# A hybrid decoder step on one Trainium2 core: the attention layer's samples on four column groups, its value projection in three rounded passes, units begun inside it

## What is computed

```python
def qkv_heads(h, pos, w_qkv, q_gain, k_gain):
    qkv = (h @ w_qkv).reshape(Bt, S, N_GROUPS, 3, N_HEADS, HEAD_DIM)   # 3 groups, 8 heads of 64
    q = rope_partial(rms_norm(qkv[:, :, :, 0], q_gain), pos)
    k = rope_partial(rms_norm(qkv[:, :, :, 1], k_gain), pos)
    return q, k, qkv[:, :, :, 2]
...
# prompt: banded causal attention per group (window, dilation) = (128,1), (512,4), (2048,16)
# sample: each of 8 sequences attends to its cached keys (128, 128 and 64 reachable per query) and 4 new ones
# both: softmax over the three groups' scores joined by their denominators, then @ w_o
```

## Time and profile before

| | us |
|---|---|
| median of 3 runs | 2732.45 (2731.07 to 2735.79) |
| the profiled execution's own time | 2726.56 |
| its span, first to last instruction | 2724.7 |
| PE busy in the span | 2538.6 (93%) |
| DVE, ACT, POOL busy | 1612.4, 947.1, 783.1 |
| mean granted TensorE clock | 0.958 of full speed |
| 680 stream tiles, 512 KB each, from issue to landing | 3.3 |
| a cached key or value tile, 1792 KB | 7.9 or 7.4 |

### The profile page before, as it was taken

How to read it: one execution, slowest core, us unless ns; L and a number is a source line. 1 busy time by engine, 2 the same in 40 slices (tenths; PEclk the granted TensorE clock), 3 DMA queues, 4 the chain that set the end, 5 groups by cost and what they waited for, 6 DMA issues and landing times.

```text
span 2724.7 us, 47969 instructions
## 1 busy us (share of the span) xinstructions
PE 2538.6 (93%) x17164; PEld 2233.2 (82%) x17164; DVE 1612.4 (59%) x3417; ACT 947.1 (35%) x1627; POOL 783.1 (29%) x586
## 2 busy tenths in 40 slices
PE   5698889999999999999699898899999999999998
PEld 2244779999999999999684334579999999999998
DVE  7999537978898433333441112247968898333333
ACT  1122334344444444444220101034344443444443
POOL 0388726840000222222440000037830000222222
PEclk7699999999999999999799897899999999999999
DMA  8463334443333544444433442034443334444444
GB/s 306 175 217 138 121 126 151 153 137 131 124 131 134 169 166 165 164 167 163 176 109 116 178 161 82 31 134 155 145 141 127 127 128 144 165 166 163 168 162 141
DMA packets 104968, 405.74 MB, mean 149 GB/s; under 512 B 12560, under 2 KB 12816, under 8 KB 101680
## 3 DMA queue, kind: packets, MB, share of 16 engines
q1 hardware_dynamic: 98064, 357.74, 38.3%
q10 hardware_dynamic: 6816, 46.91, 4.6%
HBM read 395.46 MB, written 9.14 MB: 148 GB/s over the span
## 4 chain that ended last, share of the span: by engine, by line
PE 59%; issue 22%; POOL 9%; DVE 8%; ACT 1%; DMA 0%; ACTq 0%; POOLq 0%; DVEq 0%
PE ps L1099 10%; PE ps L1091 10%; PE ps L1095 10%; POOL ring_lo L1685 7%; PE ps L1071 6%; PE ps L1070 6%; PE ps L1074 6%; PE ps L1058 5%; DVE big L1406 2%; POOL ring_lo L1692 1%; PE ps L629 1%; PE ps L969 1%; PE ps L633 1%; PE ps L636 1%; PE ps L965 1%
## 5 line engine op out<-in xcount | busy, mean ns | idle before, releaser
L298 ACT ACTIVATE wt_hi<-ring 128x1024 fp32r<-128x1024 f32 x552 | 581.0, 1053 | 318.2 <-PE ps L969 209.2
L1606 DVE TENSOR_TENSOR ring_lo<-ring,wt_hi 128x1024 fp32r<-128x1024 f32 x256 | 314.7, 1230 | 492.1 <-ACT wt_hi L298 492.1
L1703 POOL TENSOR_TENSOR split<-big,w_hi 128x288 fp32r<-128x288 f32 x256 | 208.1, 813 | 1201.7 <-PE ps L1074 603.3
L1685 POOL TENSOR_TENSOR ring_lo<-ring,wt_hi 128x1024 fp32r<-128x1024 f32 x112 | 307.9, 2756 | 127.5 <-ACT wt_hi L298 127.5
L1070 PE MATMUL ps<-split,wt_hi 128*128 128x288 f32 x1152 | 328.5, 307 | 0.0
L1071 PE MATMUL ps<-split,wt_hi 128*128 128x288 f32 x1152 | 316.1, 298 | 0.0
L1099 PE MATMUL ps<-w_hi,ring_lo 128*128 128x288 f32 x2048 | 313.1, 295 | 1.4 <-DVE ring_lo L1606 1.4
L1095 PE MATMUL ps<-split,wt_hi 128*128 128x288 f32 x2048 | 313.1, 295 | 0.3
L1091 PE MATMUL ps<-w_hi,wt_hi 128*128 128x288 f32 x2048 | 312.9, 295 | 0.0
L1099 PEld LDWEIGHTS ps<-w_hi,ring_lo 128*128 128x128 f32 x2048 | 285.4, 188 | 1.9 <-DVE ring_lo L1606 1.9
L1095 PEld LDWEIGHTS ps<-split,wt_hi 128*128 128x128 f32 x2048 | 285.4, 188 | 0.8 <-POOL split L1703 0.8
(11 more groups left out here) (276 smaller groups left out, 3724.3 us busy)
## 6 DMA issues: line engine op xcount, KB each, us to landing
ring<-in_stream SPq DMA_DIRECT2D x680, 512.0 KB, 3.3
big<-in_kc ACTq DMA_DIRECT2D x8, 1792.0 KB, 7.9
big<-in_vc ACTq DMA_DIRECT2D x8, 1792.0 KB, 7.4
out_qk<-big ACTq DMA_DIRECT2D x1, 3456.0 KB, 10.3
x_keep<-xT ACTq DMA_DIRECT2D x2, 1152.0 KB, 5.5
xT<-x_keep ACTq DMA_DIRECT2D x2, 1152.0 KB, 5.8
out_v<-big ACTq DMA_DIRECT2D x1, 1536.0 KB, 13.9
xT<-in_xT ACTq DMA_DIRECT2D x1, 1152.0 KB, 9.2
```

What stands on the lines that cost most here:

```text
L298: nc.scalar.activation(wt_hi[:, n % 2], ring[:, n % RING], ACT.Copy).then_inc(S["hi_ready"], 1)
L1606: TT(ring_lo[:, s], ring[:, s], wt_hi[:, s % 2].bitcast(F32), ALU.subtract)\
L1685: TT(ring_lo[:, s], ring[:, s], wt_hi[:, s % 2].bitcast(F32), ALU.subtract)\
L1703: TT(w_lo[:, s % 2], W[:, bass.ds(4 * i + s, 1), :].rearrange("p a t -> p (a t)"), w_hi[:, s % 2].bitcast(F32), ALU.subtract).then_inc(S[" ...
```

## The change

All in the attention layer; the reference's mathematics stays the same.

- **Start.** ACT rounds the first two weight tiles, issues 22 loads of constants (the last part of the sample mask in 16 pieces) and four key loads, and only then calls `root_mean(2)`.
- **Queries and keys.** ACT copies each bank by itself behind its tile (24 copies instead of 6), and PE waits for the one bank that it writes next. DVE still squares four banks at once.
- **Values.** The prompt's products are made in three rounded passes (`v_tile`); the low part of even tiles comes from DVE (`low_v`), of odd ones from POOL (`low_odd`). The 32 sample tokens' products stay plain and go, four at a time, to four groups of 32 columns (`v_samples`), whose four partial sums are added by one product with a constant (`v_sum`) that also puts the group's rows in place.
- **Samples.** The 128 PSUM partitions now stand for head pairs, not for sequences: the four head pairs of a batch go to four column groups (`sample_keys`, `sample_values`), the sequences lie beside each other. The values of a batch are 28 calls of 128 columns instead of 7 of 512. The new keys and values are taken once for each half; `qz` is laid out anew (`spread_q`), the result copied by ACT (`sample_out`) instead of DVE.
- **Order.** The first half's softmax, its turn, units 0 and 1 and the scores of units 2 and 3 stand inside the value tiles. The 16 units run on without a break between the halves, and the samples' batches are spread behind units 2 to 15 (`SAMPLE_AT`). PSUM banks are dealt out anew so that units, samples and values don't share any, and a fourth buffer takes the fourth key load.

```diff
-LOV = (0, GROUPS + 128)
+LOV = (0, 6 + GROUPS + 128)
+IN_ATT = 16 * 22
+SAMPLE_AT = {2: 6, 4: 7, 8: 8, 9: 9, 10: 10, 12: 11, 14: 12, 15: 13}
+VBANK = ((0, 2), (3, 5), (0, 2))
...
-        def attention_act(act, own):
+        def attention_act(act, root_mean):
             act.wait_ge(S["tile_done"], VT[0] + 128)
+            high(act, QK)
+            high(act, QK + 1)
...
+            for q in range(HP):
+                for b in range(4):
+                    act.dma_start(smaskv[32 * q + 8 * b:32 * q + 8 * b + 8, CK:SW + 96],
+                                  I["smaskv"][32 * b:32 * b + 8, CK:SW + 96]).then_inc(S["in_att"], 16)
...
-            for n in range(3):
+            for n in range(4):
                 load_kv(n)
+            root_mean(2)
...
-                nc.scalar.activation(qk[:, 4 * gs:4 * gs + 4, :], ps[:, 0:4, 0:T], ACT.Copy)\
-                   .then_inc(S["aq_copied"], 1)
...
+            for n in range(24):
+                act.wait_ge(S["tile_done"], QK + n + 1)
+                high(act, QK + n + 2)
+                nc.scalar.activation(qk[:, n, :], ps[:, n % 4, 0:T], ACT.Copy).then_inc(S["aq_copied"], 1)
+                if n >= 4 and n % 4 == 0:
+                    qk_root(n // 4 - 1)
...
             for gs in range(6):
-                if gs:
-                    pe.wait_ge(S["aq_copied"], gs)
                 for m in range(4):
+                    if gs:
+                        pe.wait_ge(S["aq_copied"], 4 * gs + m - 3)
                     qk_tile(4 * gs + m, ps[:, m, 0:T])
...
+            def v_samples(g, pr):
+                n0 = VP + 4 * g + 2 * pr
+                for n in (n0, n0 + 1):
+                    tile_wait(pe, n)
+                for j in range(4):
+                    n, z = n0 + j // 2, j % 2
+                    ins = mm(ps[32 * j:32 * j + 32, VBANK[g][1], :], modsq[:, 4 * pr + j, 256:T],
+                             ring[:, n % RING, 512 * z:512 * z + 512], start=(pr == 0), stop=(pr == 1))
+                ins.then_inc(S["v_small"], 1)
+            def v_tile(g, s):
+                n, b = VP + 4 * g + s, VBANK[g][0]
+                pe.wait_ge(S["hi_ready"], HI[0] + 280 + 4 * g + s + 1)
+                for z in range(2):
+                    w = wt_hi[:, n % 2, 512 * z:512 * z + 512]
+                    for x in (h_hi, h_lo):
+                        for a in range(2):
+                            mm(ps[:, b + a, :], x[:, 2 * s + z, 128 * a:128 * a + 128], w,
+                               start=(s == 0 and z == 0 and x is h_hi), stop=False)
...
+            def sample_keys(n):
+                hf, b = n // 8, n % 4
+                kb = kv(n).rearrange("p (q k) -> p q k", q=HP)
+                for g in range(NG):
+                    bank, c0 = (6, 0) if g == 1 else (7, KOFF[g] - 512)
+                    for q in range(HP):
+                        ins = mm(ps[32 * q:32 * q + 32, bank, c0:c0 + NK[g]], qz[:, g, hf, q, 32 * b:32 * b + 32],
+                                 kb[:, q, KOFF[g]:KOFF[g] + NK[g]], start=(b == 0 and g < 2),
+                                 stop=(b == 3 and g == 1), skip_group_check=True)
...
+            def sample_values(n):
...
+                for k in range(7):
+                    for q in range(HP):
+                        ins = mm(ps[32 * q:32 * q + 32, 6, 128 * b:128 * b + 128], pts[:, k, 32 * q:32 * q + 32],
+                                 vb[:, k, 128 * q:128 * q + 128], start=(b == 0 and k == 0), stop=False,
+                                 skip_group_check=True)
...
+            for j in range(12):
+                g, s = j // 4, j % 4
+                if j == 4:
+                    pe.wait_ge(S["aq_done"], 6)
+                    pe.wait_ge(S["qz_ready"], NG)
+                    for n in range(4):
+                        sample_keys(n)
+                    sample_new_keys(0)
+                    v_sum(0)
...
+                if s % 2 == 0:
+                    v_samples(g, s // 2)
+                v_tile(g, s)
+                if j == 0:
+                    norm(5)
+                if j == 1:
+                    spread_out(5)
+                if j == 2:
+                    rotate(5)
+                if j == 6:
+                    sample_turn(0)
+                if j == 8:
+                    v_sum(1)
+                    unit_scores(0)
+                    unit_scores(1)
+                if j == 9:
+                    sample_values(4)
+                if j == 10:
+                    unit_turn(0)
+                    unit_scores(2)
+            unit_turn(1)
+            unit_scores(3)
+            sample_values(5)
+            v_sum(2)
+            unit_pv(0)
+            for u in range(2, 16):
+                unit_turn(u)
+                if u + 2 < 16:
+                    unit_scores(u + 2)
+                unit_pv(u - 1)
+                if u in SAMPLE_AT:
+                    n = SAMPLE_AT[u]
...
+                    (sample_values if n % 8 >= 4 else sample_keys)(n)
...
+                if u == 12:
+                    sample_new_keys(1)
+                if u == 13:
+                    sample_turn(1)
+            unit_pv(15)
+            sample_values(14)
+            sample_values(15)
+            sample_new_values(1)
+            sample_fold(1)
...
+            low_v(0)
             scale_qk(5)
+            low_v(1)
             finish(5)
...
+            low_v(2)
+            sample_max(0)
+            sample_norm(0)
+            low_v(3)
+            low_v(4)
+            unit_max(0)
+            unit_max(1)
+            low_v(5)
+            for u in range(16):
+                unit_den(u)
+                if u + 2 < 16:
+                    unit_max(u + 2)
+                if u:
+                    unit_out(u - 1)
+                if u == 12:
+                    sample_max(1)
+                if u == 13:
+                    sample_norm(1)
```

More of the change, by code:

```diff
@@ L504, in unit_t @@
                     act.wait_ge(S["us_pv"], u - 1)
[L505 to L520 removed]
+                nc.scalar.activation(pt_sb[u % 2][:, 0:w], unit_turned(u)[:, 0:w], ACT.Copy)\
+                    .then_inc(S["us_cpa"], 1)
@@ new lines, in v_tile @@
+            def v_tile(g, s):
[7 more added lines that the diff above has]
+                               start=(s == 0 and z == 0 and x is h_hi), stop=False)
+                if s % 2:
+                    pe.wait_ge(S["lo_u"], LOU[0] + PRE + 24 + 2 * g + s // 2 + 1)
+                else:
+                    pe.wait_ge(S["lo_v"], LOV[0] + GROUPS + 128 + 2 * g + s // 2 + 1)
+                for z in range(2):
+                    for a in range(2):
+                        ins = mm(ps[:, b + a, :], h_hi[:, 2 * s + z, 128 * a:128 * a + 128],
+                                 ring_lo[:, n % RING, 512 * z:512 * z + 512], start=False, stop=(s == 3 and z == 1))
+                ins.then_inc(S["tile_done"], 1)
@@ new lines, in sample_new_keys @@
+            def sample_new_keys(hf):
+                for g in range(NG):
+                    c0 = NEWC - 512 + 32 * g
+                    for b in range(4):
+                        for q in range(HP):
+                            ins = mm(ps[32 * q:32 * q + 32, 7, c0:c0 + 32], qz[:, g, hf, q, 32 * b:32 * b + 32],
+                                     qk[:, 8 * g + 4 + q, 256:T], start=False, stop=(b == 3 and g == NG - 1),
+                                     skip_group_check=True)
+                ins.then_inc(S["ss_mm"], 1)
@@ L748, in sample_pv, with sample_new_values @@
-                if bb == 3:
-                    ins.then_inc(S["ss_pv"], 1)
+            def sample_new_values(hf):
+                pe.wait_ge(S["vn_copied"], NG)
+                for b in range(4):
+                    for q in range(HP):
+                        ins = mm(ps[32 * q:32 * q + 32, 6, 128 * b:128 * b + 128], pts[0:96, 7, 32 * q:32 * q + 32],
+                                 v_new[0:96, 128 * q:128 * q + 128], start=False, stop=(b == 3), skip_group_check=True)
+                ins.then_inc(S["ss_pv"], 1)
@@ L1118, in attention_dve, with low_v @@
                                nc.vector.tensor_copy)
-            v.wait_ge(S["in_att"], 80)
+            v.wait_ge(S["in_att"], IN_ATT)
+            def low_v(s):
+                n = VP + 2 * s
+                v.wait_ge(S["hi_ready"], HI[0] + 280 + 2 * s + 1)
+                v.wait_ge(S["v_small"], s + 1)
+                TT(ring_lo[:, n % 4], ring[:, n % 4], wt_hi[:, n % 2].bitcast(F32), ALU.subtract)\
+                    .then_inc(S["lo_v"], 1)
             def finish(gs):
```

376 lines of the change are left out of this document (185 added, 191 removed).

## The result

| | before | after |
|---|---|---|
| median, us | 2733.15 (4 runs) | 2582.86 (4 runs, 2582.37 to 2583.46) |
| the profiled execution's own time, us | 2726.56 | 2582.37 |
| its span, us | 2724.7 | 2580.6 |
| mean granted clock | 0.958 | 0.962 |

A forecast was written before the change was run, and what follows sets the result against it. PE's own instructions bound the value stage; sample work and a PE-DVE-ACT chain the units. Value stage and units 306 to 86 + 104 = 190, -116, +1.9: -114 us; 2726.56 - 114 = 2612.6, against the median 2618, range 2590 to 2660.

The forecast's parts named there:

- rival (e): Second PEER stage: its granted clock falls behind the denser attention layer, making the kernel slower, 2776 us; chance 0.03.
- rival (d): Units begun early in the value stage gain nothing, 15 us comes back: 2633 us; chance 0.07.
- rival (c): Value batches: 128-column products do not overlap on the groups, a batch stays at 6.2 us, 39 less saved: 2657; chance 0.06.
- The wait at the norm: Query and key tiles: PE reaches the norm before DVE's square is done, a new 1.5 us wait per group.
- the third POOL subtract: Layer start: POOL runs a third subtract right behind the second, so one more DVE modulate step waits: +2.0 us.
- The clock allowances: Low-clock time added: 7 us in the value stage (79 to 86), and units 2 to 15 taken at 104, not 90.
- the list at high clock: Units 2 to 15 priced one by one at PE's high clock: 90 us, of it units 2 to 7 28.
- rival (a): Value stage and units all at high clock, 79 + 90 us, a saving of 135: 2597 us; chance 0.15.
- The four-group calls: Value stage sample work on four column groups: key batch 1.9 us, value batch 1.9, new keys left at 3.4.
- The start: Layer start: issues ahead of ACT's root cost +4.4 us, a DVE step waiting for POOL +2.0; taken 6.4.
- The query and key tiles: Bank waits and slow tiles go, new norm waits come, two slow tiles stay: -4.5 us, between -9 and +2.
- rival (b): Units at low clock throughout, 90 + 147 us for both stages, a saving of 67: 2665 us; chance 0.12.

The follow-up runs named there:

- e4: Kernel after, with units 0 to 2 and sample 4's value batch moved behind the last value tile instead of between the tiles: 2589.5 us.
- e8: Kernel after, with all sample work from unit 2 on moved into one block behind unit 15; one execution: 2625.0 us.
- e12: Second value batch and new values moved from behind unit 4 to behind unit 6, on a kernel with plain value products, later POOL start and later norm (2575.4): 2577.8 us.
- e11: Kernel after, with the first half's second value batch and new values moved from behind unit 4 to behind unit 6: 2579.6 us.
- e1: Kernel after, with the four head pairs of the sample batches one behind the other, so successive calls write the same column group: 2609.6 us.
- e2: Kernel after, with the prompt's value tiles as plain f32 products, without their rounded copies and low-part subtracts: 2581.2 us.

## Why the prediction was wrong in size

**What held.** PE's work was the bound, and the column groups took it away; the second PEER stage did not slow (rival (e): 1.00 from 2060 to 2580 us); the units did begin inside the value tiles (rival (d), priced at 15 us; 6.7 in e4); and value products of 128 columns do overlap (rival (c)): a batch takes 1.74 us on four groups and 5.08 one group behind the other. The wait at the norm (1.5, measured 1.63), the third POOL subtract (+2.0, measured +2.0) and the rounded tile (2.84, measured 2.90 to 2.99) were sized well.

**What failed, of the 30 us that the sum missed.**

1. *The clock allowances, 7 us in the value stage and 14 in the units*, the step that failed. In the value stage the low clock cost 1.7 us in one stretch. In the units the largest part was units 2 to 7: they were taken as low mostly, 35 us where the list at high clock has 28, and took 27.7, with a granted clock of 1.00 from 1508 to 1528. The reading behind it, 0.59 where units ran without samples, did not hold everywhere: short units without samples ran low in e8 and e12 and at 1.00 in e11. So why they stayed high in the kernel after is open; that units 2 and 4 have a value batch behind them is not shown to be the reason. The list at high clock, 90 us, came within 1.3 of the measured 91.3, but by luck. The measured time holds two low stretches that the list does not. They are worth 5 to 6 us, an estimate: unit 8 took 7.81 where unit 9, with more products, took 5.50; units 13 and 14 took 15.4 together and 13.1 in e4, where the clock rose earlier; and e11's units took 84.9 in all. The list itself was too long by nearly as much: unit 12 stood at 13, with new keys at 3.4, and took 9.9. For the same reason rival (a), all high clock, came nearest (169 us for the two stages; 166.2 measured; chance 0.15) although 27 us of the units ran low.
2. *The four-group calls, 4 to 5 us in the value stage.* New keys were left at the price of one group, 3.4, and took 0.88: 96 instructions on four groups go at 9 ns each, a quarter of the old 0.035 us. Key batches were priced from a quad of 512 columns at 1.9 and took 1.5.
3. *The start, 3.5 us.* A full issue (0.485) was taken for a small mask piece and 0.68 for a key load; 0.367 and 0.51 were measured (2.4 us in all), and the issues began 1.1 us earlier against the PEER stage's end.
4. *The query and key tiles, 3.4 us.* Two slow tiles were left in (2.8); behind the norms there was none. Of the three slow tiles of before only two started at 2.29 for eight products; the third fell later in the tile, and its cost was much the same (4.9 us instead of 3.4).

Against these stand waits that the prediction's clock of the value stage had shorter: tile 2 ended 20.2 us behind the last key tile, not 17.5. The 2 us of waits that it put among tiles 4 to 7 were not there. Two of its figures don't follow from its terms, though little hangs on them: 36, 13.3 and 2 give 51.3 without the turn's 1.6, not 51.5, and the 90 us of the value stage in rival (b) have no working.

The forecast also lost 5 us by its basis: the profiled execution of before lay 6 below the median, and the prediction added these 6 to its sum, while the profiled execution after lies at its median.

The range ended at 2590, below the rival without any low clock (2597); but that rival kept the terms of points 2 to 4, which all erred to the same side.

## What to carry to other kernels

Small products that use 32 of PE's columns are worth spreading over the four column groups with neighbouring instructions on different groups, and here narrow ones gained too: a batch cost a third to a quarter of its price on one group (1.74 against 5.08 us, 1.72 against 6.22). Work for which PE has room in the waits of a chain belongs there: the samples cost under 1 us inside the units against 42 behind them. And a forecast that lists its terms at the high clock should carry the low one as a range and not as a fixed allowance: units with the same waits ran at 1.00 in one execution (e11) and at 0.66 in another (e12).

## What the runs showed of the hardware that was not expected

- 96 products of 32 columns on four groups start every 9 ns (0.88 us); on one group 24 took 0.92 us, 38 ns each with the way of the last through the array.
- Calls on different column groups overlap although other calls of the same group stand between them (keys of e1: 2.44 us a batch against 6.22 on one group), but not with seven calls of a group in a row, which also add into one place (5.08 against 1.74).
- The granted clock stood low behind idles of 2.40, 2.99 and 3.55 us in the kernel after; behind 1.3 to 2.0 us it fell in some kernels (e4, e8, e12; in e2 behind 0.90) and not in others (1.63 at every norm of the kernel after, with no slow tile behind it).
- DMA issues on ACT's queue cost 0.34 to 0.68 us each; sixteen small ones in a row 0.367.
